# A two-block kernel on one Trainium2 core: the first gate's weight rows are summed by VectorE, and TensorE only adds up the partitions

## The chip, the cores and the metric

The kernel runs on one core of a Trainium2 chip. The metric is the time of one execution on the device in microseconds (us); the median of several runs counts. Each of the core's engines follows its own list of instructions: TensorE (PE in the profile, its weight loads PEld), VectorE (DVE), ScalarE (ACT), GpSimd (POOL) and SyncE (SP), which here issues nearly all DMA transfers. They wait for one another on semaphores only.

## The reference, cut to what matters

Two transformer-like blocks over 256 tokens of width 1024, all in float32. The first block takes six vectors of 1024 from one small vector `c`; the third, `g1`, is the first gate:

```python
cond = jax.nn.silu(c)
mod = cond @ ada_w[i] + ada_b[i]
sh1, sc1, g1, sh2, sc2, g2 = jnp.split(mod[:, None, :], N_MOD, axis=-1)
h = rms_norm(x, norm_g[i, 0]) * (1.0 + sc1) + sh1
y = sb_mixer(h, sb_w_in[j], sb_w_out[j])        # attention, 16 heads of 64
x = (x + g1 * y).astype(x.dtype)
h = rms_norm(x, norm_g[i, 1]) * (1.0 + sc2) + sh2
y = hier_moe(...)                               # 32 experts, two for each token
x = (x + g2 * y).astype(x.dtype)
```

So `g1` is a product of a vector of 1024 with a matrix of 1024 by 1024, and it is needed only after the attention, when the output projection `y` is added to `x`. The second block (a feed-forward net, a mixer and another feed-forward net) follows the experts.

## The kernel before, in words

The program is written by hand, engine by engine; the order of the instructions in each engine's list is the schedule. The stages that matter, with their times in the profiled execution:

- **Projections (to 99.9 us).** Queries, keys and values are made as products of halves: the float32 weights are split into a high part (ACT, `early_high`) and a rest (DVE, `early_rest`), and PE makes three products for each (lines 2190 to 2192). The value products are the last: two column units `u`, each for two token tiles `tt`, in the PSUM banks `("v", u, tt)`. DVE copies them to `vtok` (line 1519). For `u` = 0 it first makes the rest of half 10 and afterwards that of half 11, which PE needs for the second part of the second unit.
- **Attention (99.9 to 149 us).** A software pipeline over `p` = 0 to 9, two heads to each `p`. In step `p` PE makes the scores of pair `p` (lines 2350 and 2352, banks 0 to 3, head `h` in bank `h % 4`), the suffix sums of pair `p-1` (lines 2360 and 2361) and the value products of pair `p-2` (lines 2370 and 2374). For each head ACT makes three passes (lines 1096 to 1098), DVE adds (`softplus_head`, line 1529), POOL masks (line 912), and after the suffix sums DVE takes the logs of the weights (`weight_logs`, line 1557), ACT exponentiates (line 1106) and POOL masks again. Banks 0 and 1 are first taken by the values of unit 1 and go to heads 0 and 1 when DVE has copied these.
- **Adaptive vectors.** Four of them (G1, SC2, SH2, G2) are made inside the attention. The matrix of each comes as two units of 2 MB, four of its eight rows per partition in each: partition `p`, row `k` holds row `8p + k` of the matrix. `ada(a, s)` on PE makes 8 products per unit, each of a 128x32 block (`c` copied 32 times) with 512 columns, in four column strips of the array (line 2246); the sums over `k` build up in bank 6. DVE copies the bank to `adp`, half of `gain1` (`ada_part`, line 1439), and `ada_col` on PE turns it into columns by 4 products (line 2258) into bank 7; DVE adds the bias (line 1448). G1's units are made in steps 0 and 1 and its columns in step 2, behind the first unit of SC2; SC2's in 2 and 3 with columns in 4, and SH2's in 4 and 5 with columns in 6.
- **Weight ring.** The units of the first block go through a ring of six slots of 2 MB. SP issues them in a fixed order and waits before each until the unit that lay in its slot has been used; for adaptive units that is the semaphore `ada_used`. G1's units are numbers 10 and 11; behind them come SC2 (12, 13), SH2 (14, 15), G2 (16, 17), the output projection (18, 19) and then expert weights. So unit 16 waits for unit 10, 17 for 11, 18 for 12, and so on.
- **Output projection, router (149 to 190 us).**
- **Experts (190 to about 610 us).** Their weights pass through a ring of eleven slots. SP issues a slot anew when PE has used it (line 788, for the first one line 795).
- **Second block (to the end).** Products of halves again.

`ada_col` on PE as it stands before:

```python
cols = b[:, 0:KD].rearrange("p (h q) -> p q h", h=2)
for q in range(4):
    if part is None:
        last = t.matmul(cols[:, q, :], adp[:, n % 2, P * q:P * q + P], strip[:, :, 0], start=True, stop=True)
```

Each `t.matmul` with float32 operands that are not split stands as two instructions in the trace, so 8 calls are 16 instructions.

Of the kernel before, what the change touches and what calls it, by code (L numbers as in the profile page):

```python
# [24 lines left out]
ALU = mybir.AluOpType  # L25
# [3 lines left out]
P = 128  # L29
# [3 lines left out]
KD = D // P  # L33
# [21 lines left out]
RING_A, RING_B, RING_E = 6, 3, 11  # L55
# [6 lines left out]
SH1, SC1, G1, SH2, SC2, G2 = range(6)  # L62
ADA_AT = {1: G1, 3: SC2, 5: SH2}
ADA_PARTS = [(SC1, 0), (SH1, 0), (SC1, 1), (SH1, 1), (G1, None), (SC2, None), (SH2, None), (G2, None)]
# [17 lines left out]
def plan_banks():  # L82
    plan = BankPlan()

    def transposes(j):
        for tt in range(NT):
            for half in range(2):
                plan.use(("T", j, tt, half))

    transposes(0)  # L90
    plan.use(("vectors",))
    plan.use(("squares", 0))
    def conditioning(part):
        for a in (SC1, SH1):
            plan.use(("ada", a, part), fills=0)
            plan.use(("col", a, part))

    conditioning(0)
    for u in range(4):
        if u == 2:  # L100
            conditioning(1)
        for i in range(2):
            plan.use(("qk", u, i))
    for u in range(2):
        for tt in range(NT):
            plan.use(("v", u, tt))
    for p in range(PAIRS + 2):
        if p < PAIRS:
            for h in (2 * p, 2 * p + 1):
                plan.use(("z", h), bank=h % 4, fills=2)  # L110
        if p >= 2:
            plan.use(("o", p - 2), bank=4 + p % 2, fills=0)
        if p in ADA_AT:
            plan.use(("ada", ADA_AT[p], None), bank=6, fills=0)
        if p - 1 in ADA_AT:
            plan.use(("col", ADA_AT[p - 1], None), bank=7)
    plan.use(("ada", G2, None), bank=6, fills=0)
    plan.use(("perm",), bank=7)
    plan.turn = 0
    for u in range(2):  # L120
        for i in range(2):
            plan.use(("out", u, i))
    plan.use(("out", 1, 2))
    plan.use(("logits",))
    plan.turn = 0
    transposes(1)
    for half in range(2):
        plan.use(("gate2", half), bank=7 - half)
    plan.use(("router", 1), bank=4)

    def ffn(n):
        plan.turn = 0
        for j in range(FF // 256):
            if n and not j:
                for tt in range(NT):
                    plan.use(("tok", tt), bank=tt)
                plan.use(("actT",), bank=4)
            else:
                plan.use(("gate", n, j), bank=2 * (j % 2))
                plan.use(("up", n, j), bank=2 * (j % 2) + 1)  # L140
        for i in range(4):
            plan.use(("down", n, i), bank=4 + i)

    transposes(2)
    plan.use(("cols",), bank=4)
    ffn(0)
    plan.turn = 0
    transposes(3)
    for tt in range(NT):
        plan.use(("mv", 0, tt))  # L150
    plan.use(("if",))
    for u in range(4):
        for i in range(2):
            plan.use(("cq", u, i))
            if u == 0 and i == 0:
                plan.use(("gates",))
        if u == 0:
            plan.use(("B",))
        if u == 2:
            plan.use(("uT",))  # L160
        if u == 3:
            plan.use(("Mbc", 0))
            plan.use(("Mbc", 1))
            plan.use(("Mt",))
            plan.use(("ws",))
    for tt in range(NT):
        plan.use(("mv", 1, tt))
    for u in range(4):
        for tt in range(NT):
            plan.use(("mz", u, tt))  # L170
        plan.use(("s", u))
    for u in range(2):
        for h in (2 * u, 2 * u + 1):
            for tt in range(NT):
                plan.use(("num", h, tt))
        for tt in range(NT):
            plan.use(("mo", u, tt))
    for u in range(2):
        for tt in range(NT):
            plan.use(("mgm", u, tt))  # L180
    for tt in range(NT):
        for half in range(2):
            plan.use(("sv", tt, half))
    for u in range(2):
        for tt in range(NT):
            plan.use(("mgs", u, tt))
    transposes(4)
    for u in range(2):
        for tt in range(NT):
            plan.use(("mout", u, tt))  # L190
    transposes(5)
    ffn(1)
    return plan.uses


class Chain:
# [10 lines left out]
    def link(self, ins):  # L207
        self.engine.wait_ge(self.sem, self.step(ins))
# [5 lines left out]
def build_program(nc, x_in, c_in, ada_w, ada_b, norm_g, final_g, sb_w_in, sb_w_out, moe_w_grp, moe_b_grp,  # L214
# [5 lines left out]
    with ctx:  # L220
# [37 lines left out]
        gain1 = sb("gain1", [P, D])  # L258
        ident = sb("ident", [P, P])
        ones = sb("ones", [P, P])  # L260
# [5 lines left out]
        ccol = sb("ccol", [P, 2, KD])  # L266
# [40 lines left out]
        spread = gain0[:, 640:896].rearrange("p (a n) -> p a n", a=2)  # L307
        neg_ones = gain0[:, 896:1024]
        adp = gain1.rearrange("p (a n) -> p a n", a=2)

        vec = area("vec", REST + 18944, 1456)
        vcol, acol = vec[:, 0:64], vec[:, 64:112].rearrange("p (a n) -> p a n", a=6)
# [80 lines left out]
        def slot_a(n):  # L393
            s = n % RING_A
            return ring[:, s * SLOT:(s + 1) * SLOT]
# [10 lines left out]
        wa_in = [sem(f"wa{s}_in") for s in range(RING_A)]  # L406
# [7 lines left out]
        part_s, ada_used, cols_s = sem("ada_copied"), sem("ada_unit_used"), sem("ada_columns")  # L414
# [126 lines left out]
        at_a = {u: n for n, u in enumerate(units_a)}  # L541
# [159 lines left out]
        def by_k(flat, k=KD):  # L701
            return flat.rearrange("p (k n) -> p k n", k=k)
# [698 lines left out]
        def _(dve):  # L1401
            v = nc.vector
# [82 lines left out]
            def early_rest(h):  # L1485

                dve.wait_ge(early_h, h + 1)
                v.tensor_tensor(early_half(h, ewl), early_raw(h), early_half(h, ewh).bitcast(FP32), ALU.subtract)\
                 .then_inc(early_l, 1)
# [17 lines left out]
            for u in range(4):  # L1507
                early_rest(2 * u + 2 if u else 3)
                b = await_full(dve, ("qk", u, 1))
                emptied(v.tensor_scalar(qkT[:, 4 * u + 2:4 * u + 4, :], by_k(b, 2),  # L1510
                                        DH ** -0.5 if u < 2 else 1.0, None, ALU.mult), ("qk", u, 1))
                if u:
                    early_rest(2 * u + 3)
            for u in range(2):
                if u == 0:
                    early_rest(10)
                for tt in range(NT):
                    b = await_full(dve, ("v", u, tt))
                    emptied(v.tensor_copy(vtok[:, tt, NB * u:NB * u + NB], b), ("v", u, tt))
                if u == 0:  # L1520
                    early_rest(11)

            def softplus_head(h):

# [34 lines left out]
            for p in range(PAIRS + 2):  # L1559
                for i in range(2):  # L1560
                    if 1 <= p <= PAIRS:
                        weight_logs(2 * p - 2 + i)
                    if p < PAIRS:
                        softplus_head(2 * p + i)
                if p in ADA_AT:
                    ada_part(ADA_PARTS.index((ADA_AT[p], None)))
                if p - 1 in ADA_AT:
                    ada_col(ADA_PARTS.index((ADA_AT[p - 1], None)))
                if 4 <= p < 8:
                    early_part(EARLY_QKV + (p - 4) // 2, p % 2)  # L1570
                if p >= 2:
                    n = p - 2
                    b = bank(("o", n))
                    dve.wait_ge(oh_s, n + 1)
                    emptied(v.tensor_tensor(oTl[:, n, :], b[:, 0:T], oTh[:, n, :].bitcast(FP32), ALU.subtract), ("o", n))
# [557 lines left out]
        def _(pe):  # L2133
            t = nc.tensor
# [115 lines left out]
            def ada_col(n):  # L2250

                a, part = ADA_PARTS[n]
                b = open_bank(pe, ("col", a, part))
                pe.wait_ge(part_s, n + 1)
                cols = b[:, 0:KD].rearrange("p (h q) -> p q h", h=2)
                for q in range(4):
                    if part is None:
                        last = t.matmul(cols[:, q, :], adp[:, n % 2, P * q:P * q + P], strip[:, :, 0],
                                        start=True, stop=True)
                    else:  # L2260
                        last = t.matmul(b[:, q:q + 1], adp[:, n % 2, P * q:P * q + P], strips, start=True, stop=True)
                filled(last, ("col", a, part))
# [75 lines left out]
            for p in range(PAIRS + 2):  # L2338
# [25 lines left out]
                if p >= 2:  # L2364
# [7 lines left out]
                    for g in (2 * n, 2 * n + 1):  # L2372
# [1 line left out]
                        last = t.matmul(b[po:po + DH, P:T], vtok[:, 1, DH * g:DH * g + DH], att_a[:, g % 4, T:BLK],  # L2374
                                        start=False, stop=True)
                        last.then_inc(z_o, 1)
                if p < 6:
                    ada(ADA_PARTS[4 + p // 2][0], p % 2)
                if p >= PAIRS - 1 and p <= PAIRS:
                    ada(G2, p - PAIRS + 1)  # L2380
                if p - 1 in ADA_AT:
                    ada_col(ADA_PARTS.index((ADA_AT[p - 1], None)))
            logits = bank(("logits",))

# [456 lines left out]
```

## Time and profile before

| | |
|---|---|
| runs | 1239.41, 1243.97 and 1237.8 us |
| median | 1239.41 us |
| profiled execution | 1243.44 us |
| its span, first to last instruction | 1241.7 us |
| mean granted clock of TensorE | 0.931 of full speed |
| PE busy | 1060.9 us, 85% of the span |
| PEld busy | 803.2 us, 65% |
| DVE busy | 510.9 us, 41% |
| ACT busy | 403.5 us, 32% |
| POOL busy | 45.1 us, 4% |
| read from HBM | 356 MB |

Between the span and the time of the profiled execution lie 1.7 us that no instruction shows. The shares are averages over stages that are bound by different things; what one engine's time is worth is seen from the stage.

### The profile page before, as it was taken

How to read it: one execution, taken by the hardware profiler on the slowest of the kernel's cores; microseconds unless marked ns; L12 is line 12 of the kernel's file. 1: busy time of each engine (PE TensorE's matmuls, PEld its weight loads, DVE VectorE, ACT ScalarE, POOL GpSimd, SP SyncE). 2: the span in 40 equal slices, each digit the busy share in tenths (PEclk: the TensorE clock that was granted, in tenths of full speed). 3: DMA queues.
4: the chain of work that ended last, by engine and by line, in shares of the span. 5: the costliest groups of instructions: out<-in, count | busy, mean ns of one | idle time of the engine just before them, and what ended most of it. 6: DMA issues, size and time to landing. Idle time of an engine off the chain costs nothing.

```text
span 1241.7 us, 16307 instructions
## 1 busy us (share of the span) xinstructions
PE 1060.9 (85%) x7144; PEld 803.2 (65%) x7144; DVE 510.9 (41%) x618; ACT 403.5 (32%) x487; POOL 45.1 (4%) x73
## 2 busy tenths in 40 slices
PE   7999999665656373738799999999999999999998
PEld 5895693321213130313389999889888878999986
DVE  3554641120202020202065545466844886554544
ACT  3335741000000000000064443355554535544432
POOL 2001200000000000000010000000000220000000
PEclk9999999787878786868899999999999999999999
DMA  9999899999999999999976555456454356456430
GB/s 356 305 407 351 312 367 386 430 429 426 426 429 428 428 428 427 428 425 420 401 263 194 181 204 191 146 208 226 150 190 147 128 200 220 153 188 204 181 125 34
DMA packets 112561, 358.15 MB, mean 288 GB/s; under 512 B 8404, under 2 KB 54120, under 8 KB 97896
## 3 DMA queue, kind: packets, MB, share of 16 engines
q1 hardware_dynamic: 110856, 353.63, 73.7%
q10 hardware_dynamic: 1632, 3.45, 0.8%
q8 instruction: 58, 0.95, 0.3%
q14 instruction: 15, 0.12, 0.0%
HBM read 356.01 MB, written 1.05 MB: 288 GB/s over the span
## 4 chain that ended last, share of the span: by engine, by line
PE 69%; DMA 23%; DVE 3%; SPq 2%; ACT 2%; issue 1%; POOL 0%; DVEq 0%; ACTq 0%
PE psum L2190 17%; PE psum L2192 17%; PE psum L2191 17%; DMA ring<-in_moe_w_up_dram 7%; DMA ring<-in_moe_w_down_dram 5%; DMA spare<-in_moe_w_gate_dram 5%; PE psum L2523 4%; DMA spare<-in_moe_w_down_dram 3%; DMA spare<-in_moe_w_up_dram 2%; PE psum L2563 2%; SPq L742 2%; PE psum L2510 2%; PE psum L2552 1%; PE psum L2246 1%; PE psum L2139 1%; DVE wl_stream L1751 1%
## 5 line engine op out<-in xcount | busy, mean ns | idle before, releaser
L2190 PE MATMUL psum<-hTh,wh_keep 128*128 128x256 f32 x800 | 225.3, 282 | 0.6 <-DVE hTl L1774 0.6
L2191 PE MATMUL psum<-hTl,wh_keep 128*128 128x256 f32 x800 | 224.7, 281 | 0.0
L2192 PE MATMUL psum<-hTh,wl_keep 128*128 128x256 f32 x800 | 224.7, 281 | 0.0
L1751 DVE TENSOR_TENSOR wl_stream<-ring,wh_stream 128x2048 fp32r<-128x2048 f32 x52 | 119.8, 2311 | 110.3 <-ACT wh_stream L1193 110.2
L1751 DVE TENSOR_TENSOR wl_keep<-ring,wh_keep 128x2048 fp32r<-128x2048 f32 x49 | 111.9, 2291 | 105.6 <-ACT wh_keep L1193 105.5
L2190 PEld LDWEIGHTS psum<-hTh,wh_keep 128*128 128x128 f32 x800 | 150.7, 188 | 0.9 <-issue 0.8
L2191 PEld LDWEIGHTS psum<-hTl,wh_keep 128*128 128x128 f32 x800 | 150.8, 188 | 0.0
L2192 PEld LDWEIGHTS psum<-hTh,wl_keep 128*128 128x128 f32 x800 | 150.7, 188 | 0.0
L1193 ACT ACTIVATE wh_stream<-ring 128x2048 fp32r<-128x2048 f32 x52 | 99.4, 1916 | 152.2 <-PE psum L2192 152.2
L2523 PE MATMUL psum<-spare,m_xT 128*32 128x512 f32 x416 | 90.8, 675 | 57.8 <-DMA ring<-in_moe_w_up_dram 32.4
L1193 ACT ACTIVATE wh_keep<-ring 128x2048 fp32r<-128x2048 f32 x49 | 93.5, 1919 | 123.9 <-PE psum L2192 123.3
L2523 PE MATMUL psum<-ring,m_xT 128*32 128x512 f32 x352 | 97.8, 659 | 13.9 <-DMA ring<-in_moe_w_up_dram 12.5
L2190 PE MATMUL psum<-wh_stream,hTh 128*128 128x512 f32 (+1 forms) x256 | 98.7, 385 | 0.8 <-DVE wl_stream L1751 0.8
L2192 PE MATMUL psum<-wh_stream,hTl 128*128 128x512 f32 (+1 forms) x256 | 97.1, 379 | 0.0
L2191 PE MATMUL psum<-wl_stream,hTh 128*128 128x512 f32 (+1 forms) x256 | 96.8, 378 | 0.0
L1707 DVE TENSOR_TENSOR m_h<-m_sg,psum 128x512 f32<-128x512 f32 x8 | 8.2, 1027 | 204.8 <-PE psum L2523 168.0
L2523 PEld LDWEIGHTS psum<-spare,m_xT 128*32 128x32 f32 x416 | 24.1, 123 | 99.9 <-issue 99.1
L2563 PE MATMUL psum<-ring,m_sg 128*32 128x512 f32 x288 | 55.7, 749 | 35.5 <-DMA spare<-in_moe_w_down_dram 17.9
L1149 ACT ACTIVATE m_xT<-psum,ccol 128x128 f32<-128x128 f32 x32 | 12.1, 457 | 190.9 <-PE psum L2475 190.9
L2190 PE MATMUL psum<-wh_stream,actTh 128*128 128x512 f32 x176 | 68.7, 390 | 0.0
L2191 PE MATMUL psum<-wl_stream,actTh 128*128 128x512 f32 x176 | 68.5, 389 | 0.0
L2192 PE MATMUL psum<-wh_stream,actTl 128*128 128x512 f32 x176 | 68.5, 389 | 0.0
(369 smaller groups left out, 1648.5 us busy)
## 6 DMA issues: line engine op xcount, KB each, us to landing
ring<-in_ffn_w_in_dram SPq DMA_DIRECT2D x44, 1024.0 KB, 7.7
ring<-in_moe_w_down_dram SPq DMA_DIRECT2D x18, 2048.0 KB, 37.7
ring<-in_w_mix_in_dram SPq DMA_DIRECT2D x32, 1024.0 KB, 6.7
spare<-in_moe_w_up_dram SPq DMA_DIRECT2D x14, 2048.0 KB, 34.6
ring<-in_ada_w_dram SPq DMA_DIRECT2D x24, 1024.0 KB, 14.3
ring<-in_moe_w_gate_dram SPq DMA_DIRECT2D x12, 2048.0 KB, 33.5
spare<-in_moe_w_gate_dram SPq DMA_DIRECT2D x12, 2048.0 KB, 39.4
ring<-in_moe_w_up_dram SPq DMA_DIRECT2D x10, 2048.0 KB, 36.6
```

Of the source, the lines that this page charges most:

```text
L742: sp.dma_start(dst[:, a:a + 1, :], view[:, bass.ds(e + 2 * (u % 2) + a, 1), lo:lo + 2 * D]).then_inc(landed, 16)
L1193: a.activation(dst, src, ACT.Copy).then_inc(split_h, 1)
L1751: v.tensor_tensor(split_half(h, wl), raw_half(h), split_half(h, wh).bitcast(FP32), ALU.subtract)\
L2139: t.matmul(b[:, 0:P], ident, ident, start=True, stop=True, skip_group_check=True)
L2190: t.matmul(dst, sh, mh, start=first, stop=False, skip_group_check=True)
L2191: t.matmul(dst, sh, ml, start=False, stop=False, skip_group_check=True)
L2192: return t.matmul(dst, sl, mh, start=False, stop=final, skip_group_check=True)
L2246: last = t.matmul(b[CAP * e:CAP * e + CAP, :], crep[:, 4 * s + i, :], w[:, i, NB * h:NB * h + NB], start=(s == 0 and i < 2), stop=(s == 1 ...
L2510: last = t.matmul(psum[CAP * e:CAP * e + CAP, 4 + i, :], m_xT[:, k, CAP * e:CAP * e + CAP], w[e // 2][:, e % 2, kk, :], start=(k == 0), st ...
L2523: last = t.matmul(psum[CAP * e:CAP * e + CAP, 4 + i, :], m_xT[:, k, CAP * e:CAP * e + CAP], w[e][:, k, :], start=(k == 0), stop=(k == KD - 1))
L2552: last = t.matmul(psum[CAP * e:CAP * e + CAP, 6 + half, :], m_hT[:, f, CAP * e:CAP * e + CAP], w[e // 2][:, e % 2, kk, NB * half:NB * half ...
L2563: last = t.matmul(psum[CAP * e:CAP * e + CAP, 6 + half, :], m_hT[:, f, CAP * e:CAP * e + CAP], w[e][:, f, NB * half:NB * half + NB], start ...
```

## The change

G1 no longer goes through `ada`. Instead DVE multiplies each of the eight rows that a partition holds by that partition's own value of `silu(c)` (`ccol[:, 1, k]`) and adds them up in `gate_sum`, which is all of `gain1`, 128x1024. Each of the eight steps (`gate_term`) is one DVE instruction over 1024 columns, linked: DVE waits for the end of it before it goes on. The first is a `tensor_scalar`, the others are `scalar_tensor_tensor`. They are placed around the last value products: step 0 after the copies of value unit 0, steps 1 to 5 after `early_rest(11)` and before the copies of value unit 1, steps 6 and 7 after these and before the first `softplus_head`. After steps 3 and 7 DVE counts up `ada_used`, after step 7 `part_s` as well.

PE no longer makes the 16 products of G1 in steps 0 and 1. In step 2 it makes 8 products of a 128x128 block of `gate_sum` with one column of ones, which add up the partitions; they stand ahead of SC2's first unit instead of behind it. Bank 6 is not taken for G1, and DVE makes no copy of it.

```diff
@@ plan_banks
         if p in ADA_AT:
-            plan.use(("ada", ADA_AT[p], None), bank=6, fills=0)
+            if ADA_AT[p] != G1:
+                plan.use(("ada", ADA_AT[p], None), bank=6, fills=0)
@@ buffers
         adp = gain1.rearrange("p (a n) -> p a n", a=2)
+        gate_sum = gain1
@@ vector engine
+            def gate_term(k):
+
+                n = at_a["ada", G1, k // 4]
+                dve.wait_ge(wa_in[n % RING_A], 32 * (n // RING_A + 1))
+                w, c = by_k(slot_a(n), 4)[:, k % 4, :], ccol[:, 1, k:k + 1]
+                if k == 0:
+                    link(v.tensor_scalar(gate_sum, w, c, None, ALU.mult))
+                else:
+                    link(v.scalar_tensor_tensor(gate_sum, w, c, gate_sum, ALU.mult, ALU.add))
+                if k % 4 == 3:
+                    dve.sem_inc(ada_used, 1)
+                if k == KD - 1:
+                    dve.sem_inc(part_s, 1)
+
             for u in range(2):
                 if u == 0:
                     early_rest(10)
...
                     emptied(v.tensor_copy(vtok[:, tt, NB * u:NB * u + NB], b), ("v", u, tt))
                 if u == 0:
+                    gate_term(0)
                     early_rest(11)
+                    for k in range(1, 6):
+                        gate_term(k)
+            gate_term(6)
+            gate_term(7)
...
-                if p in ADA_AT:
+                if p in ADA_AT and ADA_AT[p] != G1:
                     ada_part(ADA_PARTS.index((ADA_AT[p], None)))
@@ tensor engine, ada_col
-                for q in range(4):
-                    if part is None:
+                for q in range(KD if a == G1 else 4):
+                    if a == G1:
+                        last = t.matmul(b[:, q:q + 1], gate_sum[:, P * q:P * q + P], ones[:, 0:1], start=True, stop=True)
+                    elif part is None:
@@ tensor engine, attention loop
-                if p < 6:
+                if p == 2:
+                    ada_col(ADA_PARTS.index((G1, None)))
+                if 2 <= p < 6:
                     ada(ADA_PARTS[4 + p // 2][0], p % 2)
                 if p >= PAIRS - 1 and p <= PAIRS:
                     ada(G2, p - PAIRS + 1)
-                if p - 1 in ADA_AT:
+                if p > 2 and p - 1 in ADA_AT:
                     ada_col(ADA_PARTS.index((ADA_AT[p - 1], None)))
```

## Rows read from the trace of the kernel before

**Rows 1.** The page, busy share of the DMA engines in 40 equal slices, tenths.
```profile
DMA  9999899999999999999976555456454356456430
```

**Rows 2.** Windows: us, busy (instructions) of PE, PEld, DVE, ACT, POOL; clock, DMA share, GB/s.
```profile
140.00:150.00 10.00, 10.00 (x78) 5.14 (x77) 5.83 (x11) 5.37 (x13) 3.34 (x6) 1.00 0.49 180
...
190.00:200.00 10.00, 10.00 (x97) 3.25 (x99) 0.42 (x1) 1.51 (x4) 0.00 (x0) 1.00 0.87 300
...
210.00:220.00 10.00, 9.16 (x60) 2.95 (x52) 3.22 (x5) 0.00 (x0) 0.00 (x0) 0.97 1.03 437
```

**Rows 3.** The chain that ended last, 99 to 243 us: start, length, what.
```profile
99.89 0.70 DVE vtok L1519
...
105.86 0.91 PE psum L2360 x2
...
107.00 1.85 PE psum L2246 x16
...
112.44 1.85 PE psum L2246 x16
114.29 0.98 PE psum L2258 x8
...
206.96 5.37 PE psum L2552 x32
212.32 30.30 DMA ring<-in_moe_w_up_dram
```

**Rows 4.** PE's timeline: start, busy, what, [idle before <- releaser].
```profile
19.20 0.95 PE L2261 MATMUL psum<-vec,gain 128*128 128x1 f32 x8
...
101.58 1.92 PE L2246 MATMUL psum<-ring,gain 128*32 128x512 f32 x16
...
108.78 0.70 PE L2350 MATMUL psum<-qkT 64*128 64x256 f32 x4
...
112.37 1.92 PE L2246 MATMUL psum<-ring,gain 128*32 128x512 f32 x16
```

**Rows 5.** DVE's timeline from the last value products on.
```profile
90.70 2.29 DVE L1488 TENSOR_TENSOR ewl<-ring,ewh 128x2048 fp32r<-128x2048 f32 x1 [1.32 <-ACT ewh L1056]
97.09 0.69 DVE L1519 COPY vtok<-psum 128x512 f32<-128x512 f32 x1 [4.10 <-PE psum L2192]
...
103.29 0.56 DVE L1529 SCALAR_TENSOR_TENSOR att_sp<-psum,att_az 128x384 f32<-128x384 f32 x1 [2.70 <-ACT att_az L1098]
...
107.03 0.56 DVE L1557 TENSOR_SCALAR att_a<-psum 128x384 f32<-128x384 f32 x1 [0.21 <-PE psum L2361]
```

**Rows 6.** Groups of DVE by form: count, busy us, mean ns, idle before.
```profile
L2008 DVE TENSOR_TENSOR zv<-zv,gain_sb 128x1024 f32<-128x1024 f32 x2 | 2.4, 1224 | 0.1
L1811 DVE TENSOR_SCALAR x<-x,ss 128x1024 f32<-128x1024 f32 x2 | 1.5, 748 | 0.1
...
L1864 DVE SCALAR_TENSOR_TENSOR hn<-x,rs,gain 128x512 f32<-128x512 f32 x4 | 2.8, 749 | 0.1
```

**Rows 7.** Timeline of SP's issues, of unit 16 and of the first expert slot reissued.
```profile
103.57 0.88 SPq L774 DMA_DIRECT2D ring<-in_ada_w_dram  x2
...
192.38 2.10 SPq L795 DMA_DIRECT2D ring<-in_moe_w_down_dram  x2
```

**Rows 8.** Windows around a fall of the granted clock, and one in the attention.
```profile
203.70:207.10 3.40, 1.47 (x16) 0.57 (x12) 1.03 (x1) 0.60 (x1) 0.00 (x0) 1.00 0.97 414
207.10:210.50 3.40, 3.40 (x20) 0.88 (x18) 0.00 (x0) 0.00 (x0) 0.00 (x0) 0.50 1.01 434
...
103.30:106.70 3.40, 3.03 (x19) 1.94 (x16) 2.10 (x4) 3.24 (x8) 0.82 (x2) 1.00 0.62 186
```

**Rows 9.** Timelines of POOL and DVE: POOL's first mask; both engines at 980 us.
```profile
103.92 0.41 POOL L912 TENSOR_SCALAR_AFFINE_SELECT att_sp<-att_sp 128x256 f32<-128x256 f32 x1 [78.87 <-DVE att_sp L1529]
...
977.17 6.73 POOL L947 TENSOR_TENSOR sig_o<-sig_o,gain 128x1024 f32<-128x1024 f32 x2 [75.66 <-ACT sig_o L1339]
...
981.68 3.30 DVE L2007 TENSOR_TENSOR zv<-zv,gain_sg 128x1024 f32<-128x1024 f32 x1
```

## The prediction

> **What bounds the kernel now.** I read the page first. Its row of DMA shares stands at 9 for the first twenty of 40 slices, to about 620 us, except for one 8 [rows 1]; the tenths are too coarse to say whether the queue or an engine leads, so I went to the chain of waits. From the last value copy at 99.89 us to 212.3 us the chain runs through engines, mostly PE, and then goes over to expert weights in flight: PE's products of line 2552 at 206.96, then 30.30 us of DMA at 212.32 [rows 3]. The windows say the same from the other side: the DMA engines are at 0.49 in 140 to 150 us and at 0.87 in 190 to 200, and full from 210 on [rows 2]. The last hole ends when SP can issue the first expert slot anew, at 192.38 [rows 7]; that issue, and those after it, wait for PE. So the rest of the expert stage is a fixed number of bytes behind a moment that PE sets. A microsecond that the attention gains or loses before 190 us moves the end by one; bytes that come earlier inside the attention move nothing, because a hole still follows them.
>
> Inside the attention I looked at the chain and at PE's timeline together. From the value copy to 105.86 us the chain goes over the passes of ACT, one DVE addition and one POOL mask to PE's suffix sums of head 1, and from 107.00 on it is PE without a break until 128 us, G1's second unit in it, but not the first [rows 3]: the first unit runs at 101.58 [rows 4], while PE would have waited for ACT anyway.
>
> **What is removed.** Two units of 16 instructions. In the chain a unit takes 1.85 us [rows 3]. The first is covered by ACT's passes: worth nothing. The second is in the chain, but is not worth 1.85 us, for something is late right behind it. The scores of pair 2 need banks 0 and 1, and bank 1 is free only when DVE has ended `weight_logs(1)`, which starts at 107.03 and takes 0.56 us, to 107.59 [rows 5]. With some 0.06 us for the semaphore PE starts at 107.65 instead of 108.78 [rows 4]: 1.13 us gained. From there to the end of the value products of pair 0 it needs 112.37 - 108.78 = 3.59 us [rows 4]; POOL's masks for head 3 and weight 1 are done before PE comes to them. PE would be there at 107.65 + 3.59 = 111.24. DVE's copy of the bank (0.69 us by the value copies of the same size [rows 5]) also goes; DVE waits for PE there, so it is worth nothing.
>
> **What is added on PE.** The columns of G1 are 8 calls, 16 instructions, instead of 4 calls. Four calls with two columns took 0.98 us [rows 3], four with one column 0.95 us busy [rows 4]. Double is 1.9 to 1.96 us, or 1.76 if the tail of 0.07 us is counted only once: 1.76 to 1.96, I take 1.9. With SC2's unit (1.85) PE ends step 2 at 111.24 + 1.90 + 1.85 = 114.99. Before, the unit and the columns took 1.85 + 0.98 = 2.83 us [rows 3] from 112.37 on [rows 4], to 115.20. Net on PE: 115.20 - 114.99 = 0.2 us gained. That the columns move ahead of SC2's first unit delays the release of slot 12, and so SP's issue of unit 18, by 114.99 - 114.22 = 0.8 us (the unit began at 112.37 and took 1.85); this and everything in SP's list behind it waits for PE at each step and was not in the chain, so nothing is charged.
>
> **What is added on DVE.** One `tensor_scalar` over 1024 columns: 0.748 us by the same form elsewhere [rows 6]. It fits into the 1.32 us in which DVE waits before `early_rest(11)` [rows 5], even at the 1.28 us of its neighbours. Seven `scalar_tensor_tensor` over 1024 columns, a form that the trace does not show. The lower bound is the two-tensor operation of that size, 1.224 us; the upper is twice the 0.749 us of the same operation over 512 columns, 1.498 us [rows 6]. The doubled one counts its fixed part twice. From 512 to 1024 columns the two-tensor operation gains 1.224 - 0.69 = 0.53 us, when the copy's 0.69 [rows 5] stands for it; 0.749 + 0.53 = 1.28 us is what I take. The link adds about 0.03 us.
>
> VectorE: DVE Perf Modes of the Trainium skill (section on the errata) gives (N+151)/0.96 ns for a float32 two-tensor operation; the trace agrees for 1024 columns with 1.224 us [rows 6]. By that rule each step costs 1.22 us instead of 1.28, and the delay worked out below would vanish.
>
> Steps 1 to 5 start when `early_rest(11)` ends: 90.70 + 2.29 = 92.99 [rows 5], less 0.09 of overlap, 92.90. They end at 92.90 + 5 x 1.31 = 99.45. What is behind them on DVE are the copies of the second value unit, and behind these wait heads 0 and 1 on PE. The first copy, ready at 97.09 [rows 5], now runs from 99.48 to 100.17, the second from 100.09 to 100.78 instead of 99.89 to 100.59 [rows 3]. That is 0.2 us late, and it passes on in full: scores, ACT, DVE, POOL and PE follow each other in the chain. At 1.224 us a step the delay is 0, at 1.498 it is 1.3 us.
>
> Steps 6 and 7 take 2 x 1.31 = 2.62 us. DVE waits 2.70 us there for ACT before the first `softplus_head` [rows 5], and if that cover were short, the suffix sums of head 0 still have the wait for head 1 ahead of 105.86 in reserve. Nothing.
>
> G1's slots come free at about 97 and 103.5 us (steps 3 and 7). Unit 16 is then issued some 6 us ahead of its 103.57 [rows 7]; by the first part this is worth nothing, and it costs nothing, since G2 is used only in steps 7 and 8.
>
> **Sum without the clock.** 0.2 us gained on PE, 0.2 us lost on DVE: 0.0.
>
> **The clock.** What the first unit of G1 also did was keep PE at work. In 103.3 to 106.7 PE is busy for 3.03 of 3.40 us, and the granted clock stays at 1.00 (2.4 GHz) [rows 8]. Without it PE has the scores of two pairs until about 102.9 us, some 1.7 us of work with 64 of 128 rows, then waits for head 0 until about 104.6, makes 1.06 us of suffix sums, waits for head 1. From 103 to 106.4 it would work some 1.4 us. In the expert stage the clock went to 0.50 (1.2 GHz) at 207.1, after a stretch in which PE was busy for 1.47 of 3.40 us, and came back 3.4 us later, PE being busy throughout [rows 8]. The attention after the change looks like the stretch before that fall. If it falls, 3.4 us of PE's work take twice as long; some of it is then in the wait for head 1 or bank 1. The full price is 3.4 / 2 = 1.7 us, with those waits (about 0.35 us before 105.86, of which half is saved) 1.5 us. I hold this likelier than not, 0.55, and forecast it: 0.0 + 1.5 = 1.5 us slower.
>
> The sum stands against the profiled execution's own time: 1243.44 + 1.5 = 1244.9 us (span 1243.2 and 1.7 around it). That execution lay 4.0 us above the median of the runs shown. Against the median the forecast is 1239.41 + 1.5 = 1240.9 us.
>
> **Rivals.**
> - *The clock holds.* The time stays at 1239.4, with 0.0 from the sum. For it: the stretch from 103.3 has no single wait above 2 us, and the windows of the attention before all have a clock of 1.00 [rows 2, 8]. Against it: the stretch before the fall [rows 8]. Chance 0.25.
> - *DVE's steps are slow, and the value copies and heads wait.* At 977.17 POOL works on two tensors, and there a DVE operation over 1024 columns took 3.30 us instead of 1.22 [rows 9]. Were a step r us, the copies would be late by 5r - 6.2, and steps 6 and 7 push the first head by 2r - 2.65. To lose 0.5%, 6.2 us, r must reach 2.15; at 3.30 the loss is 10.3 + 3.95 = 14.3 us, 1253.7. Against it: POOL is idle for 78.87 us before its first mask at 103.92 [rows 9], so nothing but the end of step 7 could meet it, and just before step 1 a subtraction of 2048 columns takes 2.29 us, 1.12 ns a column [rows 5]. Chance 0.04. SBUF — State Buffer of the Trainium skill (who interferes with whom) has DVE and GpSimd lock a shared pair of ports against each other; the 3.30 us beside POOL's work fit that, and by it the steps here would be undisturbed.
> - *All of PE's G1 work counts.* If PE, and not ACT, were what the first steps wait for, both units would come off: 3.70 - 0.92 (4 more column calls) = 2.8 us less, 1236.6. The chain is against it. Chance 0.08.
> - *Earlier slots pay.* The transfers ahead of 190 us have holes, 5 us of them in 140 to 150 alone [rows 2]. If G2's earlier 4 MB let the whole stream move up, up to the 6 us of unit 16 could be saved: 1233.4. Each later issue waits for PE, though. Chance 0.03.
> - *The change doesn't do what it says:* PE's second unit is replaced by columns of nearly its length (1.13 us gained, 0.92 added). That is in the sum already.
> - *The clock falls for more than one such stretch*, at 1.5 us each: two make 1242.4. Chance 0.05, since PE is busy without a break once the suffix sums run.
>
> **Range and chances.** The low end takes the rival of PE's full work with nothing lost, 1236.6, and half a microsecond for the spread of medians: 1236. The high end takes 1.498 us a step (1.3), one more fall (3.0 in all) and 2 us of spread, which the runs shown have (1237.8 to 1243.97): 1245.7. I can't tell apart less than about 0.5%, 6.2 us, and every case but the slow DVE steps and the slots is well inside it: same 0.89, slower 0.07 (0.04 and what I may have missed behind the expert stage's own falls of the clock), faster 0.04.
>
> **What the profile after would show.** Eight DVE instructions of 128x1024, seven near 1.28 us, the first in the wait before 90.70; the last value copy at about 100.1; no product of line 2246 before the third step; 16 instructions for G1's columns in about 1.9 us at about 111.4; SP's issue of unit 16 at about 97; and a granted clock of 0.50 for some 3.4 us between 104 and 111 us, with the end of step 2 at about 116.5 (115.0 without the fall). I would be wrong if the copies end much after 100.8 us, if the chain stays on DVE in the first heads, if the clock stays at 1.00, or if a wait for a transfer shows ahead of 190 us.

## The result and the profile after

| | before | after |
|---|---|---|
| median of 22 runs | 1239.82 us | 1243.01 us |
| lowest, highest | 1237.8, 1244.88 | 1241.16, 1246.79 |
| profiled execution (its span) | 1243.44 (1241.7) | 1242.76 (1240.9) |

The ratio after to before is 1.0023, 95% interval 1.0013 to 1.0034: by it the change makes the kernel 2.9 us slower (the medians are 3.2 us apart), less than the 0.5% that I set as the bound, but clear of noise. The profiled execution of the changed kernel, however, is 0.7 us faster than that of the kernel before. The two profiles therefore show what the sum without the clock does, and not where the loss is. In the attention the granted clock stayed at 1.00 in both.

PE's timeline in the profile after, to be held against [rows 4]:

```profile
100.90 0.70 PE L2373 MATMUL psum<-qkT 64*128 64x256 f32 x4 [1.28 <-DVE vtok L1535]
...
101.63 0.63 PE L2373 MATMUL psum<-qkT 64*128 64x256 f32 x4
...
104.61 0.91 PE L2383 MATMUL psum<-att_sp,vec 128*128 128x384 f32 x2 [2.13 <-POOL att_sp L914]
...
107.91 0.70 PE L2373 MATMUL psum<-qkT 64*128 64x256 f32 x4 [0.74 <-DVE att_a L1578]
...
111.49 1.95 PE L2279 MATMUL psum<-ones,gain 128*128 128x1 f32 x16
113.37 1.92 PE L2267 MATMUL psum<-ring,gain 128*32 128x512 f32 x16
115.22 0.70 PE L2373 MATMUL psum<-qkT 64*128 64x256 f32 x4
```

The scores of pairs 0 and 1 now follow each other, then PE waits 2.13 us for head 0, makes its suffix sums and those of head 1, and waits again, 0.74 us, for bank 1. The 2.13 us are what the experiments call the hole. The columns of G1 (L2279), 16 instructions, stand ahead of SC2's first unit (L2267). The scores of pair 3 begin at 115.22; before they began at the end of the old columns, 115.20. The sum without the clock was 0.0, and the profile has 0.0.

DVE's timeline and the group of its seven sums, for [rows 5, 6]:

```profile
89.06 0.74 DVE L1522 TENSOR_SCALAR gain<-ring,ccol 128x1024 f32<-128x1024 f32 x1
90.54 2.29 DVE L1490 TENSOR_TENSOR ewl<-ring,ewh 128x2048 fp32r<-128x2048 f32 x1 [0.73 <-ACT ewh L1058]
92.75 6.67 DVE L1524 SCALAR_TENSOR_TENSOR gain<-ring,ccol,gain 128x1024 f32<-128x1024 f32 x5
99.46 1.29 DVE L1535 COPY vtok<-psum 128x512 f32<-128x512 f32 x2
100.67 2.60 DVE L1524 SCALAR_TENSOR_TENSOR gain<-ring,ccol,gain 128x1024 f32<-128x1024 f32 x2
103.51 0.56 DVE L1550 SCALAR_TENSOR_TENSOR att_sp<-psum,att_az 128x384 f32<-128x384 f32 x1 [0.25 <-ACT att_az L1100]
```

```profile
L1524 DVE SCALAR_TENSOR_TENSOR gain<-ring,ccol,gain 128x1024 f32<-128x1024 f32 x7 | 9.0, 1283 | 0.3
```

A sum over 1024 columns takes 1.283 us, five take 6.67 us with their links (the waits of each step for the end of the one before). The two copies of the second value unit run together behind them, 99.46 to 100.75, and the scores start at 100.90 instead of 100.73.

SP's issues of units 16 and 17, which stood at 103.57 [rows 7] and 108.91:

```profile
96.76 0.88 SPq L776 DMA_DIRECT2D ring<-in_ada_w_dram  x2
...
103.35 0.88 SPq L776 DMA_DIRECT2D ring<-in_ada_w_dram  x2
```

From here to the first experts the two profiles agree within 0.02 us: the first gathering of tokens starts at 186.46 against 186.47. Only then the clock makes a difference, and it is in favour of the changed kernel: in the profile before it fell at 207.1 [rows 8], in the one after it didn't, and the chain goes over from PE to the transfer at 210.61, 1.7 us earlier than before [rows 3].

```profile
206.94 3.67 PE psum L2577 x32
210.61 30.10 DMA ring<-in_moe_w_up_dram
```

### The profile page after: what moved, and what is told of

Its sections match the earlier page's. It is cut to its first block, busy times and chain, and to the rows that moved or that the text cites. A ratio compares the mean times of both kernels' runs of the same rounds, so it can differ in the third digit from the quotient of the medians.

```text
span 1240.9 us, 16272 instructions
## 1 busy us (share of the span) xinstructions
PE 1050.1 (85%) x7120; PEld 800.2 (64%) x7120; DVE 519.8 (42%) x625; ACT 403.4 (33%) x487; POOL 44.9 (4%) x73
## 4 chain that ended last, share of the span: by engine, by line
PE 67%; DMA 24%; DVE 3%; SPq 3%; ACT 2%; issue 1%; POOL 0%; DVEq 0%; ACTq 0%
PE psum L2211 17%; PE psum L2213 16%; PE psum L2212 16%; DMA ring<-in_moe_w_up_dram 10%; DMA ring<-in_moe_w_down_dram 5%; PE psum L2548 4%; DMA spare<-in_moe_w_down_dram 3%; DMA spare<-in_moe_w_gate_dram 3%; DMA ring<-in_moe_w_gate_dram 2%; PE psum L2588 2%; SPq L744 2%; PE psum L2535 2%; DMA ring<-in_sb_w_in_dram 1%; PE psum L2577 1%; PE psum L2160 1%
## 5 line engine op out<-in xcount | busy, mean ns | idle before, releaser
L1734 DVE TENSOR_TENSOR m_xT<-psum,g2b 128x512 f32<-128x512 f32 x16 | 10.3, 686 | 139.5 <-PE psum L2588 112.7
```

## The experiments

Each kernel ran 12 times beside the kernel before; a ratio is its time to that of the kernel before. "Hole" is the place in step 0 where PE's first unit of G1 was. "A fall" is a stretch with a granted clock of 0.50 (1.2 GHz).

**The kernel before and the changed kernel again.** No edit.

> The kernel before against itself. Every theory: 1.000, and the width of the interval says what 5 rounds can tell. Its profile is a second look at the same program: the profiled execution shown ahead of the prediction took 1243.44 us, 3.6 above the median of 22 runs, so this one should lie nearer 1239.8. The clock theory (the fall comes in some executions and not in others) expects the low execution to differ from the high one in the number and place of the stretches at a granted clock of 0.50, by 1.5 us or more, and not ahead of 200 us. The slot theory has nothing to say.

> The changed kernel again, for a second profile in the same job. Ratio 1.0023 as on record. Clock theory: either a granted clock of 0.50 for some 3.4 us between 104 and 111 us and the columns of G1 about 1.5 us later than in the first profile (111.5), or no such stretch in this profile as in the first; if neither profile has one, the theory is in trouble. Slot theory (the time is lost by unit 16 and 17 being issued earlier, which puts the expert transfers or the clock's pattern in another order): both engines level with the kernel before until 204.5 us, and the loss behind it.

Measured: 1.0001 (0.9988 to 1.0014) and 1.0019 (1.0005 to 1.0033). So 12 runs tell about 0.14%. The second profile of the kernel before had no fall in the attention, but its execution took 1245.46 us and not near 1239.8, and it had a fall at 24.6 us, where I had expected none ahead of 200 us. That of the changed kernel had one, right behind the hole. Windows of that second profile, in the columns of [rows 2]:

```profile
104.10:107.50 3.40, 1.27 (x8) 0.68 (x4) 2.06 (x3) 3.25 (x7) 0.55 (x2) 1.00 1.04 413
107.50:110.90 3.40, 2.37 (x7) 1.47 (x8) 2.09 (x4) 2.87 (x7) 1.07 (x3) 0.50 1.03 410
110.90:114.30 3.40, 3.40 (x13) 2.46 (x13) 0.04 (x1) 2.06 (x6) 0.76 (x2) 0.50 0.57 228
```

and PE's timeline in it:

```profile
102.68 0.70 PE L2373 MATMUL psum<-qkT 64*128 64x256 f32 x4 [1.27 <-DVE vtok L1535]
...
106.39 0.91 PE L2383 MATMUL psum<-att_sp,vec 128*128 128x384 f32 x2 [2.13 <-POOL att_sp L914]
...
107.81 1.65 PE L2383 MATMUL psum<-att_sp,vec 128*128 128x384 f32 x2 [0.29 <-POOL att_sp L914]
...
117.82 1.92 PE L2267 MATMUL psum<-ring,gain 128*32 128x512 f32 x16
```

PE is busy for 1.27 of 3.40 us ahead of the fall. Suffix sums of one head that took 0.91 us at 106.39 take 1.65 for the next head at 107.81. From the first scores to SC2's first unit it is 117.82 - 102.68 = 15.14 us here and 113.37 - 100.90 = 12.47 in the first profile: this fall of 6.8 us costs 2.67 us. (Everything starts 1.8 us later here; this profile has another fall, at 25.5 us, ahead of the changed code, as the second profile of the kernel before has.)

**Work put into the hole.** `keep_busy` multiplies the 128x128 identity matrix by itself 8 times, 16 instructions; nobody reads the result. The same kernel was measured twice.

```diff
+                if p == 0:
+                    keep_busy(open_bank(pe, ("ada", SC2, None)), 8)
                 if p == 2:
                     ada_col(ADA_PARTS.index((G1, None)))
```

> The changed kernel with 8 products of 128x128 on PE (about 1.9 us, results thrown away) in step 0, where the first unit of G1 was. Clock theory: PE stays at work, no fall, the time goes back to that of the kernel before: ratio 1.0000 (at most 1.0005). Slot theory and DVE theory: nothing changes against the changed kernel, 1.0023.

> The filled kernel again, for the interval and a second profile. Clock theory: no granted clock of 0.50 between 100 and 115 us, and 1.0000 to 1.0005. Without the clock theory: 1.0020.

Measured: 1.0010 (0.9994 to 1.0025) and 1.0003 (0.9989 to 1.0018). No fall in the attention in either profile. PE makes 2.0 us of useless products, and by the point estimates most of the loss is gone. The intervals hold 1.0000 both times; the second leaves 1.0019 and more out, the first, whose 1.0010 is twice the most that I had expected, doesn't.

**DVE's steps on top of the kernel before.** `gate_term` and its calls as in the change, `ada_used` and `part_s` left alone, and SP waits for DVE too.

```diff
+                if k % 4 == 3:
+                    dve.sem_inc(gate_seen, 1)
...
+                if n - RING_A in (at_a["ada", G1, 0], at_a["ada", G1, 1]):
+                    sp.wait_ge(gate_seen, n - RING_A - at_a["ada", G1, 0] + 1)
```

> The kernel before with the eight DVE steps added where the change has them, and their sum thrown away: PE's products of G1, their copies and columns stay, and the slots of units 10 and 11 come free only when both PE and DVE have used them, as before (about 103.5 and 109). DVE theory (the value copies 0.2 us late are all of it): 0.2 us, 1.0002; if the steps cost the 2.9 us that the change lost, 1.0023. Clock theory: PE is kept busy, 1.0002. Slot theory: unchanged release, 1.0002.

Measured: 1.0002 (0.9988 to 1.0016). In its profile the scores start at 100.81 and those of pair 3 at 115.28: 0.1 us behind the kernel before in both places. The interval leaves the change's 1.0023 out: DVE's work is not the loss.

**Work only taken away.** The kernel before; the result lacks G1's first unit. (Not shown: the second unit now opens the bank itself.)

```diff
+                if a == G1 and s == 0:
+                    pe.sem_inc(ada_used, 1)
+                    return
                 w = by_k(slot_a(n), 4)
...
```

> The kernel before with one thing left out: PE's 8 products of G1's first unit in step 0 (1.85 us). The gate's sum lacks four of eight rows of each partition. Slot 10 is released at the same place in PE's list, a little earlier (about 101.7 instead of 103.5), and DVE does nothing new. Work is only taken away, and by the chain it was never in the way. Without the clock: 0.0 us, 1.0000. Clock theory: the hole in PE's work is the one of the change, the granted clock falls in most executions and the kernel gets slower by leaving work out, by 1.5 to 2.9 us: 1.0012 to 1.0023. Slot theory: 1.7 us earlier release of one unit, at most a part of the loss.

Measured: 1.0018 (1.0003 to 1.0034). Leaving out 1.85 us of PE's work that was not in the chain makes the kernel 2.2 us slower (0.4 to 4.2 by the interval), nearly the whole loss of the change, without a DVE step or a column product being touched. Its one profile has no fall in the attention, and there the attention is as long as before: the scores of pair 3 start 116.63 - 102.16 = 14.47 us behind the first, before 115.20 - 100.73 = 14.47.

```profile
102.16 0.70 PE L2353 MATMUL psum<-qkT 64*128 64x256 f32 x4 [0.88 <-DVE vtok L1519]
...
105.81 0.91 PE L2363 MATMUL psum<-att_sp,vec 128*128 128x384 f32 x2 [2.07 <-POOL att_sp L912]
...
116.63 0.70 PE L2353 MATMUL psum<-qkT 64*128 64x256 f32 x4
```

**Slots released late.** DVE counts up `gate_seen` after step 3 instead of `ada_used`; PE releases.

```diff
+                if p == 0:
+                    pe.wait_ge(gate_seen, 1)
+                    pe.sem_inc(ada_used, 1)
+                if p == 1:
+                    pe.wait_ge(part_s, 5)
+                    pe.sem_inc(ada_used, 1)
```

> The changed kernel, but the slots of units 10 and 11 are released by PE in steps 0 and 1 (about 101.7 and 107), near where they were released before (103.5 and 108.9), instead of by DVE at 97 and 103.3. PE's work is that of the change. Slot theory: back to 1.0000. Clock theory: stays at 1.0020 to 1.0023.

Measured: 1.0019 (1.0005 to 1.0033). With the later release the loss stays. The release is not quite as late as before: units 16 and 17 are issued 0.1 and 5.2 us behind the first scores (before 2.8 and 8.2 behind them, in the change 4.1 ahead and 2.5 behind). What rules the slots out is this run together with the filled kernel, which issues unit 16 as early as the change does, 4.1 us ahead of the scores, and loses little. The profile shows a fall that I hadn't expected, not behind the hole but behind the columns of G1:

```profile
113.23 1.95 PE L2280 MATMUL psum<-ones,gain 128*128 128x1 f32 x16
115.11 3.49 PE L2268 MATMUL psum<-ring,gain 128*32 128x512 f32 x16
118.53 0.79 PE L2374 MATMUL psum<-qkT 64*128 64x256 f32 x4
```

SC2's first unit takes 3.49 instead of 1.92 us; from the first scores (102.64) to those of pair 3 it is 15.89 us against 14.32 in the first profile after: 1.57 us for a fall of 3.4 us.

**The columns in the hole.** A version meant to be better. DVE's steps 0 and 1 ahead of `early_rest(10)`, 2 behind the first value copies, 3 to 6 behind `early_rest(11)`, 7 behind the last copies; PE's columns in step 1.

```diff
+                if p == 1:
+                    ada_col(ADA_PARTS.index((G1, None)))
                 if 1 <= p <= PAIRS:
                     for g in (2 * p - 2, 2 * p - 1):
...
-                if p == 2:
-                    ada_col(ADA_PARTS.index((G1, None)))
```

> A better version, if the working is right. DVE steps 0 and 1 stand before early_rest(10), where DVE waits 3.3 us for ACT, step 2 after the first value copies, 3 to 6 after early_rest(11), and 7 after the last value copies: 4 steps of 1.31 end at 98.1, ahead of the copy at 99.9, so the 0.2 us are gone, and the sum is ready at about 101.9. G1's columns go from step 2 to step 1, behind the scores of pair 1 and ahead of the suffix sums: 102.4 to 104.3, in PE's hole. Sum without the clock: 1.9 + 0.2 us less than the change, -2.1 us against the kernel before, 0.9983. Clock theory: the hole is filled, but by products with one moving column, and whether that keeps the clock up no row has shown; with a fall 0.9995 to 1.0005, without it 0.9983.

Measured: 0.9993 (0.9982 to 1.0003), between what I had expected with and without a fall. Its profile has a fall. PE's timeline and windows there:

```profile
102.06 1.95 PE L2280 MATMUL psum<-ones,gain 128*128 128x1 f32 x16
104.20 1.44 PE L2386 MATMUL psum<-att_sp,vec 128*128 128x384 f32 x2 [0.20 <-POOL att_sp L914]
...
113.95 0.70 PE L2374 MATMUL psum<-qkT 64*128 64x256 f32 x4
```

```profile
101.10:104.50 3.40, 3.20 (x31) 3.00 (x28) 1.05 (x2) 2.90 (x7) 0.41 (x1) 0.99 1.03 410
104.50:107.90 3.40, 3.27 (x8) 1.78 (x6) 1.67 (x4) 3.27 (x8) 0.81 (x2) 0.50 1.02 406
```

Here PE is busy for 3.20 of 3.40 us and the clock falls all the same. The hole is closed in time, but by products with one moving column. This fall of 3.4 us costs less than 1 us: the scores of pair 3 start 113.95 - 100.55 = 13.40 us behind the first, in the version of the next paragraph without a fall 12.45.

**64 columns of ones instead of one.** The same 16 instructions, of whose result DVE reads one column in 64.

```diff
-                        last = t.matmul(b[:, q:q + 1], gate_sum[:, P * q:P * q + P], ones[:, 0:1], start=True, stop=True)
+                        last = t.matmul(b[:, 64 * q:64 * q + 64], gate_sum[:, P * q:P * q + P], ones[:, 0:64], start=True, stop=True)
```

Made once on the filled kernel, once on the one with the columns in the hole, once on the changed kernel with its hole (the line in which DVE picks the columns is not shown).

> The filled kernel (8 thrown-away products of 128x128 in step 0), and G1's columns made with 64 columns of ones moving instead of one, of which DVE reads one; 16 instructions as before. Two profiles had their fall elsewhere than in the hole: in the kernel with late slots it came at 115.3 us, right behind the one-column products of 113.2 to 115.1. Clock theory in two parts (hole and one-column products): both are gone here, no fall in the attention, 0.0 us, 1.0000. If only the hole counts: the same as the filled kernel, 1.0003 to 1.0010. Without the clock theory: 1.0020.

> The version with the columns in PE's hole, again with 64 columns of ones moving. Its profile with one column had the granted clock at 0.50 for 3.4 us from 104.5, right behind the columns. Without a fall the sum is -2.1 us against the kernel before: 0.9983. If the wider products make no difference to the clock: 0.9993 as with one column. A cost of the wider products themselves: 8 thrown-away products of 128 columns took 1.98 us where 8 of one column took 1.88, so at most 0.1 us.

> The changed kernel with 64 columns of ones moving in G1's column products instead of one, and the hole in step 0 left as it is. It splits the filled version with wide columns (0.9995) into its two parts, beside the fill alone (1.0010 and 1.0003). If the hole is the larger part: 1.0015 to 1.0021. If the one-column products are: 1.0000 to 1.0006. Its profile is one more with a hole: a stretch at 0.50 that begins between 104 and 111 us in half of the cases.

Measured: 0.9995 (0.9981 to 1.0009), 0.9977 (0.9966 to 0.9989), and 1.0013 (0.9998 to 1.0028). No fall in the attention in any of the three profiles. The filled one loses nothing by its point estimate. The one with wide columns in the hole is faster than the kernel before, by 2.9 us against a sum of 2.1. With the hole left open the point estimate keeps half of the loss; the interval reaches from nothing to all of it, so how the loss divides between hole and one-column products is not measured. Nor is it shown that the width helps with the columns in the hole: 0.9977 and 0.9993 have overlapping intervals. PE and DVE in the fastest version:

```profile
101.39 0.70 PE L2375 MATMUL psum<-qkT 64*128 64x256 f32 x4 [0.88 <-DVE vtok L1538]
...
102.90 2.00 PE L2281 MATMUL psum<-ones,gain 128*128 128x64 f32 x16
105.04 0.91 PE L2387 MATMUL psum<-att_sp,vec 128*128 128x384 f32 x2
...
113.84 0.70 PE L2375 MATMUL psum<-qkT 64*128 64x256 f32 x4
```

```profile
82.36 0.75 DVE L1523 TENSOR_SCALAR gain<-ring,ccol 128x1024 f32<-128x1024 f32 x1
83.15 1.28 DVE L1525 SCALAR_TENSOR_TENSOR gain<-ring,ccol,gain 128x1024 f32<-128x1024 f32 x1
...
100.55 0.69 DVE L1538 COPY vtok<-psum 128x512 f32<-128x512 f32 x1 [0.84 <-PE psum L2215]
101.16 1.28 DVE L1525 SCALAR_TENSOR_TENSOR gain<-ring,ccol,gain 128x1024 f32<-128x1024 f32 x1
```

The wide columns take 2.00 us instead of 1.95, and PE goes on with the suffix sums at full speed. The last value copy waits for PE again, 0.84 us (PE's own wait is 0.88 us as before, not 1.28), and from the first scores to those of pair 3 it is 113.84 - 101.39 = 12.45 us, against 14.47 before.

**The changed kernel a third time.**

> The changed kernel once more, for a third profile and more executions. 1.0020 to 1.0023. Of the four profiles with the hole and one-column products behind it so far (the changed kernel twice, the first unit left out, late slots) two had a fall between 100 and 120 us, of the five without a hole none. Clock theory: a fall in this one with a chance of one in two or more; and G1's hole and columns level with the first profile where there is none.

Measured: 1.0021 (1.0005 to 1.0036), and no fall in the attention (12.48 us from the first scores to SC2's first unit).

## Why the prediction was right, and what of it was off

The forecast was 1240.9 us, 1.5 us slower; measured were 2.9 us slower (1.6 to 4.2 by the interval). The side and the range held, and the loss comes from where the forecast put it, PE's emptied place in step 0. The size is in part luck: it was forecast from one certain fall of 1.5 us, and that fall did not come in every execution. The forecast's own sign of being wrong, a clock that stays at 1.00 in the attention, stood in the first profile after.

- **The sum without the clock** was 0.0 and is 0.0 in the profile. PE starts step 2 at 107.91 (107.65 and 0.2 late were forecast: 107.85), and reaches the columns at 111.49 (111.44). The columns take 1.88 us (1.9). The scores of pair 3 start at 115.22 (115.2).
- **DVE's steps:** 1.283 us against 1.28 taken; value copies to 100.75 against 100.78; scores 0.17 late against 0.2. That this is so close is luck in part: with their links five steps took 6.67 us and not 5 x 1.31 = 6.55, but they started at 92.75 and not at 92.90, because the rest of half 11 began 0.16 us earlier. The rule for two tensors of the Trainium skill (VectorE: DVE Perf Modes, the errata), 1.22 us, is for an operation without the scalar factor and would have been 0.06 us a step short. Steps 6 and 7 left 0.25 us of DVE's wait for ACT, so they hid, as forecast.
- **Slots:** unit 16 was issued at 96.76 (about 97 forecast), and it was worth nothing. The later release left the ratio at 1.0019.
- **The clock.** That the emptied place in step 0 costs more than it gives is shown by runs: taking out only PE's first unit gives 1.0018, putting useless products there takes the ratio of the change from 1.0019 to 1.0010 and 1.0003, and with wide columns to 0.9995. Taken together, each kernel compared inside its own batch, the four measurements with the hole and without wide columns (48 executions) have a mean 2.3 us above that of the kernel before, with a standard error of 0.35; the two of the filled kernel (24) 0.7 us, standard error 0.5. That the granted clock falls there is seen in one of the three profiles of the change, at 107.5 us. The record also has the mean granted clock of every execution: 0.9358 in those 48 and in the first 22 of the change, 0.9371 in the 111 executions of the kernel before in the same batches, 0.9373 in the 36 with a filled hole, each to about 0.0004. Over 1240 us, 0.0013 is at most 1.6 us of time. So the clock is lower where the hole is; the mean doesn't say in which stage, and it covers at most 1.6 of the 2.3 us.
- **The mis-sized term** is the price of the fall: "3.4 / 2 = 1.7 us, with those waits [...] 1.5 us". The fall seen behind the hole lasted 6.8 us and cost 2.67; the one of 3.4 us behind the columns cost 1.57. PE was not "busy without a break" once the suffix sums ran: with the clock at 0.50 it was busy for 2.37 of the first 3.40 us, and waited for POOL's mask of head 1 and for bank 1. A fall of that length is the rival of two stretches, priced at 3.0 us with a chance of 0.05.
- **A step that may be missing:** the columns. I priced them by time alone. Two profiles had their fall right behind the one-column products. But seven profiles have such products for G1, and in the other five no fall follows them; that they have a part in the loss is not shown.

**What stays open.** Of the six profiles that have the hole (the change three times, the first unit gone, late slots, wide columns), two have a fall in the attention, at 2.67 and 1.57 us, and only the first of these is right behind the hole. A mean over the six is 4.24 / 6 = 0.7 us, less than the 2.9 us of the ratio. Six executions are few, and in the kernels' other executions the profile doesn't say where the clock fell. Of the eight profiles without the hole one has a fall in the attention, that of the one-column products in it.

Two other places have a spread of their own. A fall ahead of 30 us stands in eight of the 14 profiles: in these the scores start at 101.39 to 103.35 us, in the others at 100.55 to 100.91. Five of the eight are profiles with the hole, though PE's work up to there is the same in all; 14 profiles can't tell that from chance. And the last group of experts, from its first gathering product to its last product, took between 49.6 and 53.2 us, of the kernel before 53.0, 53.0 and, with DVE's steps added, 49.7. So whether falls in the attention are more frequent than in these six profiles, or a part of the loss lies in such other falls, is not settled. What is shown is that the loss hangs on PE's work in the hole and not on DVE or on the slots.

## What to carry to other kernels

Ahead of moving work off TensorE, look at what that work kept running: 1.85 us of products that no chain of waits contained were worth 2.2 us (0.4 to 4.2) by being there. Put the next useful work into the hole instead, and look at the granted clock behind it; here the same sum, with its columns in the hole and 64 moving columns, turned 0.23% slower into 0.23% faster. And take more than one profile before and after: the first pair had the changed kernel 0.7 us ahead, while 22 runs had it 2.9 us behind.

## What the runs showed of the hardware that I had not expected

- Column products with one moving column keep PE busy by the profile, but the granted clock fell to 0.50 right behind them in two of the seven profiles that have them for G1: at 104.5 us after PE had been busy for 3.20 of 3.40 us, and at 115.3 us after 3.40 of 3.40. With 64 moving columns, at 2.00 instead of 1.95 us, no fall followed in three profiles. So a busy PE was no guard against a fall; that the one column is the reason is not shown by so few.
- The same program has the fall in one execution and not in the next: in one profile of the change at 107.5 us, in two others not, though PE's work and waits up to there, counted from the first scores, agree within 0.01 us.
- What a fall costs depends on the waits around it. With PE busy for 2.37 + 3.40 = 5.77 of 6.8 us it cost 2.67 us, with PE busy throughout 3.4 us it cost 1.57, both somewhat under half of PE's busy time; the one at 104.5 us cost 0.95 with PE busy for 3.27 of 3.40, where part of the slower work took the place of waits (the wait of 0.35 us for head 1 in the version without a fall is gone in it).
